# Zeroing, normed tiles and the gates' logs reordered at a layer's beginning, and rotation's addition a step later, in a two-block hybrid transformer kernel

## The reference

```
z = rms_norm(x, g) @ w_in        # 16 q heads, 2 k and 2 v heads of 64, and the mLSTM's columns
q, k = rms_norm per head, then rotation of the first 16 of 64 dims:
       x1*cos - x2*sin, x2*cos + x1*sin
ya = attention in a band of 128, 16 meta tokens always seen, a sink logit per head
log_i = z_i + b_i ; log_f = log_sigmoid(z_f + b_f)     # the gates, 4 heads
hm = mlstm_chunkwise(silu(conv(mq, mk)), mv, log_i, log_f)
x = x + concat(ya * silu(ag), rms_norm(hm) * sigmoid(mo) * silu(mgate)) @ w_out
```

## Time and profile before

| | |
|---|---|
| time, median of 3 runs | 3083.72 us (3081.52 to 3089.0) |
| time of the profiled execution | 3080.72 us |
| span in the profile | 3078.7 us |
| TensorE busy | 2941.4 us, 96% |
| VectorE, ScalarE busy | 1622.7 us (53%), 1264.2 us (41%) |
| GpSimd busy | 188.5 us (6%) |
| mean granted TensorE clock | 0.984 of full |

### The profile page before, as it was taken

One profiled execution on the slowest core, in us unless ns is written; L12 is line 12 of the kernel. 1 busy time (PEld: TensorE's weight loads), 2 busy tenths in 40 slices (PEclk: granted clock), 3 DMA queues, 4 the chain that ended last, 5 costly groups with the idle time before them and its releaser, 6 DMA issues.

```text
span 3078.7 us, 44915 instructions
## 1 busy us (share of the span) xinstructions
PE 2941.4 (96%) x18366; PEld 2565.8 (83%) x18366; DVE 1622.7 (53%) x3259; ACT 1264.2 (41%) x2640; POOL 188.5 (6%) x207
## 2 busy tenths in 40 slices
PE   8899999988999999999999999999999999999998
PEld 6788888978989889888888877887888888877886
DVE  5666645347674453676433554325677433554334
ACT  4455423244554232466333433223566333433222
POOL 3100000020000000100000000000100000000000
PEclk9999999998999999999999999999999999999999
DMA  3111322211113222322232222333322242222332
GB/s 113 45 44 58 105 68 69 83 45 44 58 57 105 75 75 84 115 84 68 83 118 88 81 70 70 95 96 100 117 80 69 82 123 83 83 69 80 92 95 82
DMA packets 99735, 250.24 MB, mean 81 GB/s; under 512 B 8597, under 2 KB 44845, under 8 KB 99274
## 3 DMA queue, kind: packets, MB, share of 16 engines
q1 hardware_dynamic: 99530, 247.37, 25.3%
HBM read 239.60 MB, written 6.50 MB: 80 GB/s over the span
## 4 chain that ended last, share of the span: by engine, by line
PE 80%; DVE 11%; ACT 4%; issue 2%; DMA 1%; POOL 1%; SPq 0%; DVEq 0%; POOLq 0%; ACTq 0%
PE ps L92 78%; PE ps L95 3%; ACT Z L98 2%; DVE cl L101 2%; DVE Z L101 2%; DVE Z L109 1%; DVE ZR L101 1%; DVE stat L122 1%; DMA st<-in_stream_dram 1%; DVE Z L119 1%; DVE Z L105 1%; ACT ch L98 1%; ACT L98 0%; POOL stat L101 0%; DVE stat L109 0%
## 5 line engine op out<-in xcount | busy, mean ns | idle before, releaser
L92 PE MATMUL ps<-hh,ch 128*128 128x512 f32 (+1 forms) x2624 | 804.7, 346 | 41.0 <-DVE cl L101 18.5
L92 PE MATMUL ps<-hl,ch 128*128 128x264 f32 (+1 forms) x2816 | 833.7, 339 | 0.0
L92 PE MATMUL ps<-hh,cl 128*128 128x512 f32 (+1 forms) x2624 | 793.9, 342 | 0.0
L101 DVE TENSOR_TENSOR cl<-st,ch 128x1024 fp32r<-128x1024 f32 (+1 forms) x436 | 495.7, 1152 | 535.6 <-ACT ch L98 535.2
L98 ACT ACTIVATE ch<-st 128x1024 fp32r<-128x1024 f32 (+1 forms) x436 | 424.4, 990 | 353.2 <-PE ps L92 326.5
L92 PEld LDWEIGHTS ps<-hh,ch 128*128 128x128 f32 x2624 | 453.8, 190 | 113.4 <-issue 27.5
L92 PEld LDWEIGHTS ps<-hl,ch 128*128 128x128 f32 x2816 | 485.2, 190 | 59.2
L92 PEld LDWEIGHTS ps<-hh,cl 128*128 128x128 f32 x2624 | 454.4, 190 | 59.3
L98 ACT ACTIVATE Z<-ps 64x128 f32<-64x128 f32 (+7 forms) x506 | 216.7, 437 | 595.8 <-PE ps L92 469.7
L92 PE MATMUL ps<-ZR,ch 128*128 128x264 f32 (+2 forms) x1856 | 444.6, 336 | 5.5 <-DVE cl L101 5.1
L92 PEld LDWEIGHTS ps<-ZR,ch 128*128 128x128 f32 x1856 | 304.0, 189 | 48.8 <-issue 12.8
(11 more groups left out here) (133 smaller groups left out, 3224.3 us busy)
## 6 DMA issues: line engine op xcount, KB each, us to landing
st<-in_stream_dram SPq DMA_DIRECT2D x372, 512.0 KB, 3.5
st<-in_stream_dram SPq DMA_DIRECT2D x64, 256.0 KB, 3.3
Z<-decay_rows SPq DMA_DIRECT2D x8, 904.0 KB, 6.4
Z<-bias_lines SPq DMA_DIRECT2D x16, 448.0 KB, 4.2
ya_spill<-Z SPq DMA_DIRECT2D x8, 512.0 KB, 4.6
Z<-ya_spill SPq DMA_DIRECT2D x2, 2048.0 KB, 7.5
Z<-in_x_dram SPq DMA_DIRECT2D x4, 512.0 KB, 5.5
Z<-in_mem_dram SPq DMA_DIRECT2D x2, 1024.0 KB, 6.8
```

The source lines that it names most:

```text
L92: return Ins(self, self.e and self.e.matmul(o, a, b, start=start, stop=stop, skip_group_check=True))
L101: return Ins(self, self.e and self.e.tensor_tensor(o, a, b, op))
```

## The change

Five edits, all in the hybrid layers, twice each:

- GpSimd's zeroing becomes a step of its own, `vz`, ahead of all normed tiles. It keeps its waits. It stood in `vtr`, behind the last normed tile.
- The normed tiles stand earlier: 0 to 3 ahead of v's projection, 4 and 5 around v's scaling, 6 and 7 ahead of q0. They stood as 0 and 1, 2, 3, 4, and 5 to 7 behind q0.
- The gates' logs (`gra`) come behind the first of three value tiles ahead of the scores, `grf` 0 and 1 behind the second and third. They stood in steps 0, 1 and 2. `grf` 2 to 7 stand in steps 1 to 6 (3 to 8 before), `grt` in step 3 (5 before).
- The addition of the rotation goes from `rope` to the beginning of `ropeq`, one stage later, for q. k keeps it in `rope`.
- For q2 to q7, chain is called once more, ahead of the projection: the first tile of a pair is summed before the second is projected, and has its `rope` directly behind that projection.

```diff
             else:
+                chain()
                 self.proj(("q", l, t), nid, L, u, t % 2)
             chain()
             put("qkev", l, t)
...
         st["turn"].append((8, None, 0))
-        self.norms(nid, 0, 1)
+        put("vz", l)
+        self.norms(nid, 0, 1, 2, 3)
         self.projr(("v", l), nid, u, 1)
-        self.norms(nid, 2)
+        self.norms(nid, 4)
         g = self.ng()
         put("vev", l, g)
+        self.norms(nid, 5)
         chain()
-        self.norms(nid, 3)
         put("gr", l)
         if l == 0:
             put("linest")
         u = self.unit(1, l, 0)
-        self.norms(nid, 4)
+        self.norms(nid, 6, 7)
         qk(0, u)
-        self.norms(nid, 5, 6, 7)
         put("vtr", l, g)
...
         for a in range(3):
             fill(a - 3)
+            if a == 0:
+                put("gra", l)
+            else:
+                put("grf", l, a - 1)
             chain()
         for s in range(35):
             if s < 32:
                 put("sA", l, s)
-            if s == 0:
-                put("gra", l)
-            if 1 <= s < 9:
-                put("grf", l, s - 1)
-            if s == 5:
+            if 1 <= s < 7:
+                put("grf", l, s + 1)
+            if s == 3:
                 put("grt", l)
...
             def rope(l, t, n):
                 r, q = ROT[n % 2], QF[t % 3]
                 dve.wait_ge(("rotl", n), ("tk",))
-                dve.tensor_tensor(r, r, SIN, ALU.mult).then_inc("dve_rope")
-                dve.wait_ge(dve.newest, ("ropec", l, t))
+                dve.tensor_tensor(r, r, SIN, ALU.mult).then_inc("dve_rope", ("rots", n))
+                if t == 8:
+                    ropesum(l, t, n)
+
+            def ropesum(l, t, n):
+                r, q = ROT[n % 2], QF[t % 3]
+                dve.wait_ge(("rots", n), ("ropec", l, t))
                 dve.tensor_tensor(q, q, r, ALU.add).then_inc("dve_rope", ("qr", l, t), ("rotfree", n))
 
             def ropeq(l, t, n):
                 q = QF[t % 3]
+                ropesum(l, t, n)
                 dve.wait_ge(("qr", l, t), ("line",), *bars(("b1", l)))
...
-            def vtr(l, g):
+            def vz(l):
                 pool.wait_ge(("line",), *bars(("b1", l)))
                 pool.memset(VS.bitcast(F32), 0.0)
                 pool.memset(zr(7040, 512).bitcast(F32), 0.0).then_inc("pool_ones", ("zero", l))
```

More of the change, by code:

```diff
@@ L2652, in final @@
                 rsqrt(so[:, 8:12], 1024, ("so2",))
-            do = dict(sqa=sqa, dqkev=dqkev, dex=dex, hsc=hsc, memprep=memprep, dnorm=dnorm, final=final, nrml=nrml, load=load, rope=rope, qsum=qsum, vtr=vtr, mvones=mvones, pn=pn, bar=pool.bar)
+            do = dict(sqa=sqa, dqkev=dqkev, dex=dex, hsc=hsc, memprep=memprep, dnorm=dnorm, final=final, nrml=nrml, load=load, rope=rope, qsum=qsum, vz=vz, mvones=mvones, pn=pn, bar=pool.bar)
             for kind, *a in steps:
```

## The result

The changed kernel takes 3091.85 us in the median of 20 runs (3086.41 to 3098.54), the kernel before 3084.11 in 20 runs beside them (3079.96 to 3089.0): a ratio of 1.0024 [1.0017, 1.0031], some 7.7 us slower. I had forecast 3080.1 us, 3.6 less than before, in a range from 3071 to 3087. The profiled execution has a span of 3089.6 us.

The account below looks back on a forecast made before the run. TensorE, busy 96% of the span, was taken as the bound, so only its idle or low-clock time could go. Layer 1's -4.3 and layer 0's +0.75 made -3.6 us: 3080.1 us from the median 3083.7, range 3071 to 3087.

Parts of the forecast that it names:

- the zeroing in layer 0: Layer 0's head: GpSimd's fills wait for the bias line and hold its lows and k's cosine, +6.85 us.
- Rival 1: Layer 0's head: the bias line does not hold GpSimd; sum -10.5 us, 3073.2; chance 0.12.
- the logs: Gates' logs ahead of the scores: tile 0's maximum +3.07 us in layer 1, first conv projection -0.6.
- Rival 2: Ahead of tile 0: VectorE is not held for the logs, both layers keep 3.07 us; 3074.0; chance 0.12.
- Head of layer 1: -2.0 us: Layer 1 before the scores: ScalarE copies v earlier, TensorE's first sum at 64.55 for 66.56.
- From there the gains are free: Behind q2's projection, up to step 9: shorter sums and fewer waits; tile 9 -5.2 us in layer 0, -4.5 in layer 1.
- rival 3: Steps 4 to 9 give less: only step 5's 1.32 and 0.8 us are won; 3085.0; chance 0.18.
- 6.2 and 5.4: Most that layers 0 and 1 could gain: windows of 42.08 and 41.34 us with 35.9 of TensorE work at full clock.
- fourth rival: Pairs of q: the low part, ahead of the next mean squares, waits for ScalarE's copy; up to +14.4 us, 3098; chance 0.08.
- the two later pairs: Steps 12 to 24: mean squares later, a 1.2 us low-part wait gone; -0.9 us in layer 0, +0.2 in layer 1.

Follow-up runs that it names:

- e1: The changed kernel with GpSimd's zeroing put back behind q0's projection, ahead of `vtr`: 3085.57 us for 3083.87 before, ratio 1.0006.
- e5: e1 with GpSimd's first odd low part made to wait for VectorE's low part of tile 4: 3083.34 us for 3085.17 before, 0.9996.
- e2: The changed kernel with the bias line's transfer put ahead of k's rotation in SyncE's queue: 3087.22 us, ratio 1.0006 to the kernel before.
- e7: The kernel before with the gates' edits and, of the rotation's, only the addition put one stage later: 3090.65 us for 3085.17, 1.0017.
- e4: The kernel before with the gates' edits alone (`gra`, `grf`, `grt`): 3081.52 us, ratio 0.9995.
- e9: The kernel before with the normed tiles' order alone changed: 3082.62 us for 3084.0, ratio 0.9991.
- e6: The kernel before with the gates' edits and, of the rotation's, only the extra chain call for q2 to q7: 3083.44 us for 3085.17, 0.9997.
- e3: The kernel before with the rotation's two edits alone (later addition and extra chain call): 3084.75 us, ratio 1.0001.
- e8: The kernel before with the gates' edits, the normed tiles' new order and GpSimd's odd lows late, no rotation edit: 3079.75 us for 3085.17, 0.9984.
- e10: The kernel before with GpSimd's zeroing alone put ahead of the normed tiles: 3088.12 us for 3084.0, ratio 1.0009.

## Why the prediction was wrong

**Right: the zeroing in layer 0.** Forecast +6.85 us against layer 1's head. v's low part was +5.03 against a forecast of +4.85. By e1 the place of the zeroing costs 5.6 us; the difference to 6.85 is the collision that layer 0 is spared while GpSimd stands (1.35, e5). e2 shows the mechanism. Rival 1 falls.

**Right: the logs.** From v's low part to tile 0's maximum the changed kernel takes 5.4 and 4.8 us more, for 5.07 forecast (3.07 and the head's 2.0). e7, with the addition behind the gate rows as I had it there, gives +5.1 in both layers; e4 shows that 3.2 of it are the logs' and 1.9 the addition's (3.8 and 1.3 in layer 1). The 4.26 us at tile 1 are gone, and the 1.32 stand in step 3. The table load costs what its row shows (1.28). Rival 2 falls (3.16 us of wait in the row at 88.08).

**Wrong: "Head of layer 1: -2.0 us".** It was +1.1. I priced GpSimd's steps beside VectorE's work (1.8 us for 1.3), but VectorE's as they stand when GpSimd is idle (0.69 for a normed tile). The collision costs 1.35 us (e5, e9), and 1.1 to 1.3 come from the rotation's transfers landing late (3.29 for 1.97 us). e9, e2 and e5 do not show that late landing, the changed kernel and e1 do; what delays it stays open, as no run changed the transfers of that moment alone. The remaining 0.45 is the difference of e5's -1.55 to my -2.0.

**Wrong: "From there the gains are free"** (steps 3 to 9, -5.2 and -4.5; from q2's projection -5.6 and -4.9). Measured from q2's projection to tile 11: -2.7 and -2.0. That is rival 3 in size; its reason, VectorE's load in each step, was not tested. By the windows, up to tile 7's scores the gain is 0.8 us for 2.3 forecast. q2's projection ran 0.75 us longer, at 0.71 of the clock for 0.79. The bank was still waited for (2.24 us for 2.38), since q3's mean squares, which free it, came only 0.8 us earlier behind the start of q2's projection (26.46 for 27.25). Up to tile 8 it is 1.3 for 4.2: tile 7's stretch, 5.5 us of work, took 6.88 at 0.75. I had read the low clock of the old window (0.74) as belonging to the wait of 1.87 us ahead of it, and removed both. The wait went, and the low clock stood behind the wait that was left. The kernel before could have told me. In its layer 1 there is no wait of 1.87, and the clock is low behind the bank's wait of 2.40 us:

```profile
745.58:749.58 4.00, 4.00 (x18) 3.22 (x19) 1.75 (x5) 0.67 (x3) 3.22 (x2) 0.50 0.00 0
```

The bounds that I set beside the forecast (6.2 and 5.4) were wrong too, though nothing hung on them. Of the 35.9 us of work at full clock the three stretches at 1.00 (17.63 and 5.51 before, tile 8's 5.14 after) leave 7.6 for q2's projection, which took only 7.27 at 0.79.

**Open: what the rotation's two pieces are worth together.** I forecast a gain from them (q2's sum ahead of q3's projection, the wait of 1.87 us gone). Each alone is told apart beside the gates' edits: the addition costs 6.9 and 3.2 us at tile 26 (e7 less e4), the extra call gives 0.0 and 1.0 (e6 less e4). Both on the kernel before give 0.5 and 0.1 there (e3). But e5 has both and e8 neither, the rest being equal, and there the marks speak for them (tile 26 -5.6 and -2.3 for -3.7 and -2.5, so 1.7 us over both layers) and the ratios against (0.9996 for 0.9984, 3.7 us), with intervals that overlap. No run settles it. My fourth rival named the low part as what would hold the pairs. In the changed kernel, which has the extra call, the two later pairs lose nothing in layer 1 and some 0.3 us in layer 0 for -0.9 forecast, so it did not come about there; without the call it did (e7).

The rows show one price of the extra call, and it is the collision again. GpSimd's power of q2's sum, first in the changed kernel, then before:

```profile
145.59 4.62 POOL L101 TENSOR_TENSOR stat<-stat,par 128x10 f32<-128x10 f32 x1 [57.34 <-DVE stat L105]
```

```profile
141.32 1.95 POOL L101 TENSOR_TENSOR stat<-stat,par 128x10 f32<-128x10 f32 x1 [59.94 <-DVE stat L105]
```

It now starts beside VectorE's two weight conversions and the sine, which last from 145.44 to 148.3, and it ends 1.9 us behind them. The cosine that follows (150.18, 1.31 us) meets the first small VectorE instruction of tile 6 (150.54), which takes 0.96 us for the 0.22 of the next one, ahead of q3's mean squares. (Before, 0.24 us were lost in this way.) The 4.62 us stand in both layers of the five kernels with the gates' edits and the extra call (changed, e1, e2, e5, e6), and 1.95 in the other eight. For q4 and q6 it is 2.86 us with the call and 1.95 without. That these VectorE instructions are what held GpSimd is read from the times; no run moved them.

**The sum.** Layer 0: +5.2 for +0.75, of which 0.4 are missing at q2's projection, 2.9 in steps 4 to 11, 1.2 in the pairs. Layer 1: +0.9 for -4.3, of which 2.4 at q2's projection and 2.9 in steps 4 to 11. Both layers were to gain from the same terms, so their errors add. The stall of layer 0, which needed the gains beside it to come out even, came as forecast and stood alone. That the mixer layers took 3.3 us more in the profiled execution is not explained by anything here; executions of one kernel differ by up to 12 us (the changed one's, 3086.41 to 3098.54).

## What to carry to other kernels

Before an instruction goes early in an in-order queue, write down what it waits for and through which other queue that has to pass: here a transfer behind five others in SyncE's queue held GpSimd, and either moving the zeroing back or the transfer ahead took the ratio from 1.0024 to 1.0006. When VectorE work with two SBUF inputs is moved, lay GpSimd's work beside it at its new time and add the whole instruction of the other, both ways. An instruction that sits in idle time of its engine is free where it is; ask what stands ahead of it at the new place. And do not count a low clock as gone with the wait ahead of it while another wait remains: here it stood behind the one of 2.24 us that was left.

## What the runs showed that I had not expected

The granted clock falls behind waits of 1 to 2.4 us, and not each time: behind the same two waits (1.03 and 1.25 us) it was 0.72 in e4 and 1.00 before, worth 1.25 us. The wait for the bank at the first pair lasts 2.2 to 2.4 us in fourteen places (both layers of before, changed, e1, e2, e5, e9 and e10); in the 5 us behind it the clock is 0.50 to 0.69 in eight of them and 1.00 in six. Gains of about a microsecond at a step thus come and go by the clock alone, which is also why marks of single profiles (layer 1 of e2, +2.72) and medians order the kernels only roughly. And four small transfers from SBUF to SBUF landed 1.97 us after the start of their last issue before and 3.29 after, in the same place of the same layer; in layer 0 the changed kernel's were not late.
